# Third attention span of a decoder step: compact 32x32 scores, probabilities turned by VectorE

## What is computed

```python
for g, (win, dil) in enumerate(DILATED_GROUPS):
    o, lse = banded_attention(to_strided(qs[g], dil), to_strided(ks[g], dil),
                              to_strided(vs[g], dil), win // dil)
    outs.append(from_strided(o, n, dil))
    lses.append(from_strided(lse, n, dil))
y = merge_groups(outs, lses)          # softmax over the three lse, weighted sum
```

## Time and profile before

| | before |
|---|---|
| median of 3 runs | 1453.23 us (1446.16 to 1453.51) |
| profiled execution | 1452.32 us, span 1450.4 us |
| TensorE matmul busy | 1340.9 us, 92% of the span |
| VectorE, ScalarE, GpSimd busy | 782.1, 639.7, 490.9 us |
| mean granted TensorE clock | 0.966 of full speed |

### The profile page before, as it was taken

The page is one execution under the profiler, slowest core; times in us unless marked ns, Lnnn a source line. Parts: engine busy times, 40 slices in busy tenths (PEclk is TensorE's granted clock), DMA queues, the critical chain, the costliest instruction groups (busy, mean ns, idle before and its releaser), DMA issues. The chain is left out here.

```text
span 1450.4 us, 29701 instructions
## 1 busy us (share of the span) xinstructions
PE 1340.9 (92%) x11026; PEld 1287.5 (89%) x11026; DVE 782.1 (54%) x1479; ACT 639.7 (44%) x1421; POOL 490.9 (34%) x414
## 2 busy tenths in 40 slices
PE   4999999999999999999989895799999988988986
PEld 3999999999899999999979895788988978878986
DVE  4444435454335444355462045576979679686344
ACT  3243433343334434343334334376676665654332
POOL 2455323454324543245452313003334143152011
PEclk9999999999999999999999997799999999999998
DMA  5584333653235633367431162434445626623241
GB/s 161 135 229 110 96 104 94 191 150 97 79 109 157 174 91 103 82 186 224 102 85 45 52 201 77 125 98 133 137 136 153 192 65 190 191 69 112 73 154 73
DMA packets 313415, 182.62 MB, mean 126 GB/s; under 512 B 75232, under 2 KB 302256, under 8 KB 312880
## 3 DMA queue, kind: packets, MB, share of 16 engines
q1 hardware_dynamic: 313264, 180.64, 43.8%
HBM read 155.01 MB, written 46.41 MB: 139 GB/s over the span
## 5 line engine op out<-in xcount | busy, mean ns | idle before, releaser
L1321 POOL TENSOR_TENSOR wlo<-w,whi 128x1024 fp32r<-128x1024 f32 x96 | 229.8, 2394 | 455.2 <-ACT whi L993 455.2
L844 PE MATMUL at_proj<-uhi,whi 128*128 128x272 f32 x1536 | 337.4, 301 | 10.1 <-POOL ulo L1327 3.9
L844 PE MATMUL at_proj<-uhi,wlo 128*128 128x272 f32 x1536 | 320.8, 291 | 0.0
L844 PE MATMUL at_proj<-ulo,whi 128*128 128x272 f32 x1536 | 320.3, 290 | 0.0
L993 ACT ACTIVATE whi<-w 128x1024 fp32r<-128x1024 f32 x96 | 101.7, 1059 | 366.8 <-PE at_proj L844 340.0
L844 PEld LDWEIGHTS at_proj<-uhi,whi 128*128 128x128 f32 x1536 | 242.6, 192 | 14.1 <-issue 7.0
L844 PEld LDWEIGHTS at_proj<-ulo,whi 128*128 128x128 f32 x1536 | 244.9, 191 | 0.0
L844 PEld LDWEIGHTS at_proj<-uhi,wlo 128*128 128x128 f32 x1536 | 243.2, 191 | 0.0
L1789 PE MATMUL sd_proj<-uhi,whi 128*128 128x272 f32 x768 | 171.2, 305 | 8.2 <-DVE ulo L2213 3.6
L1789 PE MATMUL sd_proj<-uhi,wlo 128*128 128x272 f32 x768 | 162.3, 293 | 0.0
L1789 PE MATMUL sd_proj<-ulo,whi 128*128 128x272 f32 x768 | 161.8, 293 | 0.0
(11 more groups left out here) (300 smaller groups left out, 2344.5 us busy)
## 6 DMA issues: line engine op xcount, KB each, us to landing
w<-in_attn_w_in_dram SPq DMA_DIRECT2D x88, 512.0 KB, 4.3
w<-in_ssd_w_in_dram SPq DMA_DIRECT2D x40, 512.0 KB, 4.3
w<-in_attn_w_out_dram SPq DMA_DIRECT2D x16, 512.0 KB, 4.1
sd_h<-in_state_ssm_dram SPq DMA_DIRECT2D x16, 512.0 KB, 6.5
sd_bc<-acs_p SPq DMA_DIRECT2D x16, 512.0 KB, 5.3
out_s_ssm_dram<-sd_h SPq DMA_DIRECT2D x16, 512.0 KB, 3.2
w<-in_ssd_w_out_dram SPq DMA_DIRECT2D x16, 512.0 KB, 3.9
at_k_cache<-in_cache_kv_w_dram SPq DMA_DIRECT2D x384, 16.0 KB, 2.8
```

Of the source, the lines that this page charges most:

```text
L844: last = pe.matmul(proj[:, r, h, 0:HALF], a[:, r, kk * P:(kk + 1) * P], b[:, kk, h * HALF:(h + 1) * HALF], start=(kk == 0 and a is whi and ...
L1321: pool.tensor_tensor(wlo[:, r], w[:, r], whi[:, r].bitcast(F32), ALU.subtract).then_inc(wlo_ready, 1)
```

## The change

The third span's scores are made only where they count. For each of the four blocks of 128 queries, TensorE issues four matmuls of 32 queries by 32 keys; the query rows of the c-th go to partitions 32c to 32c+31, all in 32 columns: a score item fills 128 of the bank's 512 columns. Mask, maximum, exponential and scaling of this span work on 128 columns. Its four transposes and ScalarE's copy are gone. In their place VectorE transposes the compact 128x128 tile in 32x32 blocks (`compact_t`) and multiplies it, broadcast over four copies, by a 0/1 table (`member`) into a block-diagonal 128x512 tile `wide`, which `weigh` reads as it read `probs_t`. The item is now called `PW`, holds no PSUM bank and issues nothing on TensorE but `weigh(n - 1)`.

```diff
-HEADS = [("PT", h, w, u) for h in range(NH) for w, u in SLOT]
+HEADS = [("PW" if w == 2 else "PT", h, w, u) for h in range(NH) for w, u in SLOT]
...
+TURNED = [n for n, item in enumerate(HEADS) if item[0] == "PT"]
+ATTN = Plan(ATTN_AHEAD, ATTN_BEHIND, TILES, 2, ("OS", "OT", "KT", "PW"))
...
                     for j, (qt, kt) in enumerate(UNITS[w_][u]):
-                        last = pe.matmul(b[:, j * P:(j + 1) * P], q[:, h, qt * P:(qt + 1) * P],
-                                         k[:, kt * P:(kt + 1) * P], start=True, stop=True)
+                        if w_ < 2:
+                            last = pe.matmul(b[:, j * P:(j + 1) * P], q[:, h, qt * P:(qt + 1) * P],
+                                             k[:, kt * P:(kt + 1) * P], start=True, stop=True)
+                            continue
+                        for c in range(4):
+                            at = slice(qt * P + SQ * c, qt * P + SQ * (c + 1))
+                            last = pe.matmul(b[SQ * c:SQ * (c + 1), SQ * j:SQ * (j + 1)], q[:, h, at], k[:, at],
+                                             start=True, stop=True)
...
             def weigh(g, n):
 
                 _, h, w_, u = HEADS[n]
-                pe.wait_ge(probs_t_ready, len(HEADS) * g + n + 1)
+                if w_ == 2:
+                    pe.wait_ge(wide_ready, NH * g + h + 1)
+                    x = wide[:, h % 2]
+                else:
+                    pe.wait_ge(probs_t_ready, len(TURNED) * g + TURNED.index(n) + 1)
+                    x = probs_t[:, TURNED.index(n) % 2]
...
-                    small_item(st, g, item)
-                    if item[0] == "PT" and item != HEADS[0]:
+                    if item[0] != "PW":
+                        small_item(st, g, item)
+                    if item[0] in ("PT", "PW") and item != HEADS[0]:
                         weigh(g, HEADS.index(item) - 1)
...
                         elif item[0] == "PT":
-                            n = HEADS.index(item)
-                            act.wait_ge(head_done, len(HEADS) * g + max(n - 1, 0))
+                            n = TURNED.index(HEADS.index(item))
+                            act.wait_ge(head_done, len(HEADS) * g + (TURNED[n - 2] + 1 if n >= 2 else 0))
...
+            def widen(g, h):
+
+                dve.wait_ge(scaled_ready, len(HEADS) * g + HEADS.index(("PW", h, 2, 0)) + 1)
+                dve.transpose(compact_t[:, :], probs[:, h, SLOT[2, 0], 0:P]).then_inc(compact_ready, 1)
+                dve.wait_ge(compact_ready, NH * g + h + 1)
+                dve.wait_ge(head_done, len(HEADS) * g + (HEADS.index(("PW", h - 2, 2, 0)) + 1 if h >= 2 else 0))
+                dve.tensor_tensor(wide[:, h % 2].rearrange("p (i r m) -> p i r m", i=4, r=4),
+                                  blocks(compact_t[:, :], 4).unsqueeze(2).broadcast_to([P, 4, 4, SQ]),
+                                  member[:, 1].unsqueeze(1).unsqueeze(3).broadcast_to([P, 4, 4, SQ]), ALU.mult) \
+                    .then_inc(wide_ready, 1)
...
-    masks = np.stack([z(j >= i), z(j <= i), z((j // 32 == i // 32) & (j % 32 <= i % 32))], 1)
+    masks = np.stack([z(j >= i), z(j <= i), z(j <= i % 32)], 1)
```

More of the change, by code:

```diff
@@ L582 @@
 }
-HEADS = [("PT", h, w, u) for h in range(NH) for w, u in SLOT]
+HEADS = [("PW" if w == 2 else "PT", h, w, u) for h in range(NH) for w, u in SLOT]
 ATTN_BEHIND = {
     0: [("OT", 0), ("PC", 1), ("PN", 1)],
-    1: [("OS", 1), ("PT", 0, 0, 0), ("PT", 0, 0, 1), ("PT", 0, 1, 0), ("PT", 0, 2, 0)],
-    2: [("OT", 1), ("PT", 1, 0, 0), ("PT", 1, 0, 1), ("PT", 1, 1, 0), ("PT", 1, 2, 0), ("PT", 2, 0, 0), ("PT", 2, 0, 1),
+    1: [("OS", 1), ("PT", 0, 0, 0), ("PT", 0, 0, 1), ("PT", 0, 1, 0), ("PW", 0, 2, 0)],
+    2: [("OT", 1), ("PT", 1, 0, 0), ("PT", 1, 0, 1), ("PT", 1, 1, 0), ("PW", 1, 2, 0), ("PT", 2, 0, 0), ("PT", 2, 0, 1),
         ("PT", 2, 1, 0)],
-    3: [("PT", 2, 2, 0), ("PT", 3, 0, 0), ("PT", 3, 0, 1), ("PT", 3, 1, 0), ("PT", 3, 2, 0)],
+    3: [("PW", 2, 2, 0), ("PT", 3, 0, 0), ("PT", 3, 0, 1), ("PT", 3, 1, 0), ("PW", 3, 2, 0)],
 }
 SCORES = [item for t in range(TILES) for item in ATTN_AHEAD[t] if item[0] == "S"]
-ATTN = Plan(ATTN_AHEAD, ATTN_BEHIND, TILES, 2, ("OS", "OT", "KT"))
+TURNED = [n for n, item in enumerate(HEADS) if item[0] == "PT"]
+ATTN = Plan(ATTN_AHEAD, ATTN_BEHIND, TILES, 2, ("OS", "OT", "KT", "PW"))
 def attention_phase(nc, uhi, ulo, ident, ring, part, yg, w_in_dram, w_out, tables, caches, y_dram, p_kv, s_kv):
@@ L629, in attention_phase @@
         probs_t = m.sb("probs_t", [P, 2, 512])
+        compact_t = m.sb("compact_t", [P, P])
+        wide = m.sb("wide", [P, 2, 512])
         k_cache = m.sb("k_cache", [P, 2, 4, CW])
@@ L678, in attention_phase @@
         probs_t_ready = m.sem("probs_t_ready")
+        compact_ready = m.sem("compact_ready")
+        wide_ready = m.sem("wide_ready")
         head_done = m.sem("head_done")
@@ L952, in weigh @@
                     last = pe.matmul(strided(out_t[h % 2][:, :], w_, qt), v_rows[:, w_, kt, :],
-                                     square(probs_t[:, n % 2, j * P:(j + 1) * P], w_),
+                                     square(x[:, j * P:(j + 1) * P], w_),
                                      start=(SLOT[w_, u] == 0 and j == 0), stop=(SLOT[w_, u] == 3 and j == 3),
@@ L999, in exps @@
                 blocks = UNITS[w_][u]
+                cols = SQ if w_ == 2 else P
                 for qt in dict.fromkeys(b[0] for b in blocks):
                     js = [j for j, b in enumerate(blocks) if b[0] == qt]
-                    x = probs[:, h, SLOT[w_, u], js[0] * P:(js[-1] + 1) * P]
+                    x = probs[:, h, SLOT[w_, u], js[0] * cols:(js[-1] + 1) * cols]
                     last = act.activation(x, x, ACT.Exp, bias=neg_top[:, w_, qt, h:h + 1], scale=SCALE,
@@ L1109, in stage @@
                         elif item[0] == "PT":
-                            n = HEADS.index(item)
-                            act.wait_ge(head_done, len(HEADS) * g + max(n - 1, 0))
+                            n = TURNED.index(HEADS.index(item))
+                            act.wait_ge(head_done, len(HEADS) * g + (TURNED[n - 2] + 1 if n >= 2 else 0))
                             cols = len(UNITS[item[2]][item[3]]) * P
                             copied(st, item, probs_t[:, n % 2, 0:cols], bank(st, item)[:, 0:cols], probs_t_ready,
-                                   len(HEADS) * g + n + 1)
+                                   len(TURNED) * g + n + 1)
                     if st.head is not None:
@@ L1156, in mask_and_top @@
                 else:
-                    last = dve.tensor_tensor(blocks(dst, 4), blocks(b[:, :], 4),
-                                             masks[:, w_, :].unsqueeze(1).broadcast_to([P, 4, P]), ALU.add)
+                    cols = SQ if w_ == 2 else P
+                    last = dve.tensor_tensor(blocks(dst[:, 0:4 * cols], 4), blocks(b[:, 0:4 * cols], 4),
+                                             masks[:, w_, 0:cols].unsqueeze(1).broadcast_to([P, 4, cols]), ALU.add)
                 last.then_inc(masked_ready, 1)
@@ L1164, in mask_and_top @@
                 else:
-                    tops = [(0, 4, 0, 512)]
+                    tops = [(0, 4, 0, 4 * SQ if w_ == 2 else 512)]
                 for a, z, lo, hi in tops:
@@ L1249, in get_factors, with scale @@
                 free(dve, st, ("F",))
-            def scale(n):
+            def widen(g, h):
[7 more added lines that the diff above has]
+                    .then_inc(wide_ready, 1)
+            def scale(g, n):
                 _, h, w_, u = HEADS[n]
@@ L1256, in scale @@
                 else:
-                    parts = [(0, 4, 0, 512)]
+                    parts = [(0, 4, 0, 4 * SQ if w_ == 2 else 512)]
                 for a, z, lo, hi in parts:
@@ L1262, in scale @@
                 last.then_inc(scaled_ready, 1)
+                if w_ == 2:
+                    widen(g, h)
             def gate(g, h):
@@ L1295, in stage @@
                             for n in range(6):
-                                scale(n)
+                                scale(g, n)
                         elif item[0] == "OT":
                             sample_gate(g, item[1])
-                        elif item[0] == "PT":
+                        elif item[0] in ("PT", "PW"):
                             n = HEADS.index(item)
                             if n + 5 >= 6 and n + 5 < len(HEADS):
-                                scale(n + 5)
+                                scale(g, n + 5)
                             if n % 4 == 1 and n > 4:
```

## The result

The changed kernel took 1439.90 us in the median of 10 runs (1435.43 to 1448.39), the kernel before 1449.07 us (1444.52 to 1453.69, 10 runs). The ratio is 0.9939, 95% interval 0.9922 to 0.9956: 8.8 us less (6.4 to 11.3), where 8.6 us were forecast. The median lies inside the range of 1437 to 1454.

The account below looks back on a forecast made before the run. TensorE was taken to bound the attention, so all was costed as its time: scores -3.6, transposes -7.6, new wait +2.6, together -8.6 us, giving 1444 us. The range was 1437 to 1454 us.

Parts of the forecast that it names:

- Scores: Third span's 16 score items on TensorE: 0.58 us each instead of 0.81, saving 3.6 us.
- The edge: TensorE's loss entering and leaving a small-matmul score item, from and to the projection: 0.15 us per item.
- The other bound, 37.4 ns: Score records at the first sample item's pitch: 1.35 us an item, 16 lose 8.6 us.
- the two rivals of a floor per instruction: Small score matmuls bounded per instruction: 37.4 ns a record, 1456 us, chance 0.13; or 101 ns, 1488 us, chance 0.06.
- The prediction's estimate of 25 ns: About 60 cycles of overhead per score matmul at 2.4 GHz: 0.95 us an item, sum -2.7 us; under the 0.13 rival.
- The issue cost of about 62 ns per matmul: Score matmuls at this cost: 2.0 us an item, 1470 us; cited under the slower floor rival, chance 0.06.
- Transposes: Third span's transposes leave TensorE, four items per group: 1.91 us per group, 7.6 us saved over four groups.
- The wait in their place: TensorE waits 0.43 us for ScalarE's copy at `weigh(2)` and `weigh(14)`; less `weigh(15)`'s 0.21 us, net 2.6 us over four groups.
- VectorE's work: Scaling, transpose and widening cost at most 2.06 us per item instead of 0.80, hidden by distance to the `weigh`.
- The statistics: TensorE's wait of 1.0 us for the merged statistics in the attention was taken as unchanged.
- The weights: TensorE's 2.0 us of waits for the weights' low halves were read in the attention; no term was given.
- The clock: Rival: thinner TensorE work brings more lower-clock stretches of 2.45 us; two give 1449, three 1451; within 0.5%, chance 0.22.

Follow-up runs that it names:

- the exchanged loops: Changed kernel with the compact scores' two loops exchanged, four matmuls to one group of 32 partitions in a row; ratio 0.9964 to the kernel before.
- The reordered kernel: Changed kernel with the third span's item moved from fourth to third place in its head; ratios 0.9917 and 0.9925 to the kernel before.
- Three more widenings: Changed kernel with VectorE's multiplication into `wide` done four times over, each behind the one before; ratio 0.9943 to the kernel before.
- the three traces of the changed kernel: Changed kernel unaltered, traced in its first run and two repeats beside other kernels; ratios 0.9939, 0.9929 and 0.9946 to the kernel before.
- transposes-alone kernel: Changed kernel with the third span's scores put back to full 128x128 blocks, only its transposes moved to VectorE; ratio 0.9952 to the kernel before.

## Why the prediction was right

**Scores: right, the term too small.** On record were 0.58 us an item and 3.6 us in all. It is 0.39 + 0.10 = 0.49 us, and 16 x 0.32 = 5.1 us. The 13.5 ns a record of the second sample item carried over, and came out somewhat lower (12.1 now). The edge was charged 0.15 us; it is 0.10. The other bound, 37.4 ns, did not apply. The prediction had set it aside because its moving operand has up to 256 columns; that this is the reason for 37.4 ns was not tested. Of the two rivals of a floor per instruction neither came, and the exchanged loops show what a record costs when neighbours work in the same group: 25.9 ns. A quarter of the 101 ns of a 128-column record gives the same, so whether that is a floor per instruction or a cost that goes with the columns is not shown. The prediction's estimate of 25 ns, from the overhead in the Trainium skill, page TensorEngine Tiling, section Instruction Overhead, fits the 25.9 ns within a group if a record counts as a matmul; it does not fit across groups, where 12.1 ns were reached. The issue cost of about 62 ns per matmul, which the Trainium skill, page TensorE: Matmul & The Clock Gate, Part 1, gives for one way of decoding, is not seen: the records of these items are 12.1 and 25.9 ns apart. (The prediction called the 37.4 ns half of it; they are 0.6 of it.)

**Transposes: right.** 7.6 less 2.6 us were forecast, 5.0. The stretches from a group's first transpose on became 5.3 us shorter in all, in the changed kernel and in the one with this part alone; that kernel's ratio is worth 7.0 us (4.7 to 9.4). 64 transposes are gone.

**The wait in their place: right in place and size.** 0.43 us were forecast at `weigh(2)` and at `weigh(14)`. The eight pairs of the first trace take 1.76 to 1.91 us where 1.40 is work, 14.68 us together, so 3.5 us of waiting (forecast 3.4). Some 0.7 us at `weigh(15)` went in return. The reordered kernel, in which another item hides the copy, does without these waits and has 1.7 us less in the same stretches. The 0.16 us between the copy's end and `weigh` are a matter of counting: the first weight load starts 0.05 us behind the copy (766.75 behind 766.11 + 0.60 in the last group), and the rest is lost in the first matmul, which takes 0.38 us instead of 0.28.

**VectorE's work: hidden, as argued.** Three more widenings per item cost nothing. The prediction's bounds for the turn and the widening, 628 and 800 ns, are 312 and 735 ns.

**The statistics: not as taken.** The wait was to stay as it was; it went from 1.0 us to 1.7, 2.5 and 2.1 us in the three traces of the changed kernel.

**The weights: a term that was missing.** The prediction read the 2.0 us of waiting for the low halves of the weights and gave the change no part in them. They went, all but 0.4 us in one trace of three.

**The clock: present, not decisive.** The projection behind `F` in the second group is again the slow one. This rival had been given the outcome of no change; over three comparisons (0.9939, 0.9929, 0.9946) the gain holds. In the first pair of traces the attention holds 10.2 us at a granted clock of 0.50, both before (376.3 to 383.1 and 564.0 to 567.4) and after (369.7 to 376.5 and 540.4 to 543.8), so the clock does not explain the gain there.

**The sum.** The profiled executions differ by 16.9 us, twice the gain, and the attention of the first trace ended 12.9 us sooner. The projection's matmuls are the same in both traces, so the k-th of one can be set beside the k-th of the other, and each difference placed. 1.7 us lie ahead of the first score item of all, where the change does nothing; the transposes-alone kernel has 1.2 us there too. 5.1 us are the scores, 5.3 us the transposes with their waits, and 1.8 us the waits for the weights. The other stretches, the statistics and the projection around them above all, took 1.0 us more. That makes 12.9.

So what the prediction had terms for, 8.6 us, measured 10.4 in the attention, and 1.8 us came that it had not. The medians give 8.8 us (6.4 to 11.3), and the ratios of the other two comparisons 10.3 and 7.8 us. Whether some of the attention's gain is lost behind it, or the one trace of the kernel before is untypical, the runs don't settle. That the forecast met the measured 8.8 us to 0.2 is luck in part: the scores term was 1.5 us too small, the waits for the weights were left out on one side and the longer wait for the statistics on the other, and an interval of 2.4 us to either side can't tell 8.6 from 10.4.

## What to carry to other kernels

Cost a TensorE-bound change from start to start, between the matmuls on either side, and look in the trace for the very form of instruction that the change issues: the nearest by partitions and columns was right here, and one that shared its line was off by three times. Small matmuls with 32 weight columns pay when neighbours go to different groups of 32 partitions; the same matmuls group by group cost twice as much. And when an item is taken out of a chain, ask what it was hiding: the transposes covered a copy on another engine, which then showed, and which a change in the order of items covered in part. And when one pair of traces differs by more than the gain, set the instructions that both kernels share side by side, and read each term from the stretch between them: this gave the terms to 0.1 us, where whole executions scatter by some 10 us.

## What the hardware showed beyond that

- Fp32 matmuls of 32 weight columns on 32 moving columns: 12.1 ns a record with the four partition groups in turn, 25.9 ns with one group four times in a row. Going over to such matmuls from the projection and back costs TensorE 0.10 us more than an item of 128x128 fp32 matmuls does.
- A `weigh` that waits for ScalarE's 512-column copy starts its first weight load 0.05 us behind the copy's end, and its first matmul takes 0.1 us longer: 0.16 us of TensorE's time in all.
- VectorE's transpose of a 128x128 fp32 tile in 32x32 blocks took 312 ns, that of 448 columns 628 ns.
- One unchanged part of the program, 640 us long, differed by 6.6 us between traces of kernels that change only what stands ahead of it.
